# One transformer-style program: the first modulation's weights split into two float32r parts throughout, squares summed in pairs on GpSimd, five key units mixed into the start

## The reference, cut to what matters

```python
silu_c  = silu(c)                    # c: 1 x 2048
silu_cc = silu(c_ctx)[None]
mod_l = split(silu_c  @ w_mod + b_mod, 6)      # w_mod: 2048 x 12288, float32
mod_c = split(silu_cc @ w_mod + b_mod, 6)
hl = modulate(rms_norm(x,   norm1_g), mod_l[0], mod_l[1])
hc = modulate(rms_norm(ctx, norm1_g), mod_c[0], mod_c[1])
zl  = hl @ w_in + b_in                         # 256 x 13312
zkv = hc @ w_in[:, K_OFF:G_OFF] + b_in[K_OFF:G_OFF]   # keys and values of the context
```

## Time and profile before

| what | value |
|---|---|
| median of 3 runs | 2806.58 us (2803.66 to 2813.95) |
| the profiled execution, its own time | 2808.74 us |
| its span | 2806.9 us |
| mean granted TensorE clock | 0.981 |
| TensorE busy | 2705.8 us (96%), 21438 matmuls |
| VectorE busy | 1914.6 us (68%) |
| ScalarE busy | 1269.0 us (45%) |
| GpSimd busy | 188.1 us (7%) |

### The profile page before, as it was taken

One profiled execution on the slowest core, in us unless ns is written; L12 is line 12 of the kernel. 1 busy time (PEld: TensorE's weight loads), 2 busy tenths in 40 slices (PEclk: granted clock), 3 DMA queues, 4 the chain that ended last, 5 costly groups with the idle time before them and its releaser, 6 DMA issues.

```text
span 2806.9 us, 51478 instructions
## 1 busy us (share of the span) xinstructions
PE 2705.8 (96%) x21438; PEld 2581.1 (92%) x21438; DVE 1914.6 (68%) x2951; ACT 1269.0 (45%) x1827; POOL 188.1 (7%) x180
## 2 busy tenths in 40 slices
PE   7999999899999999999999999999999998979996
PEld 4599977798999999999999999999999998979996
DVE  6765667789998777875555645677566656487564
ACT  5522344553444545544443434464444444444453
POOL 0000011000014000100000000030000000220011
PEclk9999999999999999999999999999999999989998
DMA  8766633456876777776555555554344443535563
GB/s 310 270 229 222 204 115 112 143 188 205 273 239 223 248 265 263 258 255 205 183 191 183 181 192 183 188 187 152 135 155 146 151 150 128 175 104 180 181 200 108
DMA packets 163991, 539.02 MB, mean 192 GB/s; under 512 B 31024, under 2 KB 35120, under 8 KB 163632
## 3 DMA queue, kind: packets, MB, share of 16 engines
q1 hardware_dynamic: 163760, 535.73, 57.3%
HBM read 533.57 MB, written 2.10 MB: 191 GB/s over the span
## 4 chain that ended last, share of the span: by engine, by line
PE 62%; DVE 5%; issue 1%; ACT 1%; POOL 0%; POOLq 0%; ACTq 0%; DVEq 0%
PE ps L531 20%; PE ps L536 19%; PE ps L533 19%; DVE lo L1570 1%; DVE row L2137 1%; PE ps L865 0%; DVE AL L2213 0%; PE ps L887 0%; PE ps L888 0%; PE ps L569 0%; DVE H L2221 0%; DVE ON L2145 0%; DVE Z L2301 0%; PE ps L960 0%; PE ps L959 0%
## 5 line engine op out<-in xcount | busy, mean ns | idle before, releaser
L986 ACT ACTIVATE hi<-raw 128x1024 fp32r<-128x1024 f32 x856 | 902.0, 1059 | 954.3 <-PE ps L536 463.2
L531 PE MATMUL ps<-AH,hi 128*128 128x256 f32 (+2 forms) x4480 | 1283.5, 287 | 13.7 <-DVE AL L2213 13.7
L536 PE MATMUL ps<-AH,lo 128*128 128x256 f32 (+2 forms) x4480 | 1270.4, 284 | 9.5 <-DVE lo L1570 9.5
L533 PE MATMUL ps<-AL,hi 128*128 128x256 f32 (+2 forms) x4480 | 1269.4, 283 | 0.0
L1570 DVE TENSOR_TENSOR lo<-raw,hi 128x1024 fp32r<-128x1024 f32 x856 | 1036.0, 1224 | 201.3 <-ACT hi L986 198.9
L531 PEld LDWEIGHTS ps<-AH,hi 128*128 128x128 f32 x4480 | 850.4, 190 | 45.8 <-issue 34.6
L536 PEld LDWEIGHTS ps<-AH,lo 128*128 128x128 f32 x4480 | 849.9, 190 | 12.3 <-DVE lo L1570 12.3
L533 PEld LDWEIGHTS ps<-AL,hi 128*128 128x128 f32 x4480 | 851.2, 190 | 1.0
L531 PE MATMUL ps<-YH,hi 128*128 128x256 f32 (+1 forms) x1536 | 433.8, 282 | 6.5 <-DVE YL L2148 6.5
L536 PE MATMUL ps<-YH,lo 128*128 128x256 f32 (+1 forms) x1536 | 432.9, 282 | 0.0
L533 PE MATMUL ps<-YL,hi 128*128 128x256 f32 (+1 forms) x1536 | 432.5, 282 | 0.0
(11 more groups left out here) (253 smaller groups left out, 2493.2 us busy)
## 6 DMA issues: line engine op xcount, KB each, us to landing
raw<-in_w_ff SPq DMA_DIRECT2D x256, 512.0 KB, 4.1
raw<-in_w_in SPq DMA_DIRECT2D x208, 512.0 KB, 4.4
raw<-in_w_mod SPq DMA_DIRECT2D x192, 512.0 KB, 4.7
raw<-in_w_ain SPq DMA_DIRECT2D x128, 512.0 KB, 3.6
raw<-in_w_pin SPq DMA_DIRECT2D x64, 512.0 KB, 3.5
raw<-in_w_o SPq DMA_DIRECT2D x32, 512.0 KB, 4.7
raw<-in_w_aout SPq DMA_DIRECT2D x32, 512.0 KB, 3.5
raw<-in_w_pout SPq DMA_DIRECT2D x32, 512.0 KB, 4.3
```

The source lines that it names most:

```text
L531: e.matmul(b.ap[:, o], hi[:, k, :], xh, start=start and k + i == 0, stop=False, skip_group_check=many)
L533: e.matmul(b.ap[:, o], hi[:, k, :], xl, start=False, stop=False, skip_group_check=many)
L536: mm = e.matmul(b.ap[:, o], los[j % NSPLIT][:, k, :], xh, start=False, stop=stop and k == KU - 1, skip_group_check=many)
L986: e.activation(his[u % NSPLIT][:, :, :], raws[raw_at[i]][:, :].rearrange("p (k m) -> p k m", k=KU), ACT.Copy).then_inc(s_hi, 1)
```

## The change

1. `WHOLE` and the way `mod0` are gone: all 64 blocks of the first modulation are split in hi and lo and go through L639's form (L625 after the change). Every raw buffer of the start is freed by VectorE's `lo`.
2. GpSimd adds, for x and for ctx, the second square to the first and the fourth to the third (128x1024 each, new semaphore `s_sqa`). TensorE sums eight k tiles in place of sixteen. The place of the sums in TensorE's order moves from after the 6th to after the 10th block for x, and for ctx to after the 17th; the roots and reciprocals move with them.
3. `NLEAD` goes from 4 to 5 and `NEARLY` from 48 to 40: after 40 blocks w_in 40, 8 blocks, w_in 41, 8 blocks, w_in 42, 8 blocks, w_in 43, w_in 44, then the second halves of 40 to 44. The fifth unit accumulates in the bank `TB`, which the value transposes use later. `NSTART` is 69.

```diff
-WHOLE = (2, 5)
-NEARLY, NLEAD = 48, 4
+NEARLY, NLEAD = 40, 5
 NSTART = 64 + NLEAD
-FIRST = 64 - 8 * len(WHOLE) + NLEAD
+FIRST = NSTART
...
-    mod0 = [("mod0" if q in WHOLE else "mods", nb, q) for nb in MOD0 for q in range(8)]
+    mod0 = [("mods", nb, q) for nb in MOD0 for q in range(8)]
...
+        acc_kv = acc + [TB] + [acc[i % 4] for i in range(11)]
...
@@ TensorE, norms
-                    for _ in range(6 - 3 * c):
+                    for _ in range(9 - 3 * c):
                         yield
                     opened(xb)
-                    for k in range(16):
+                    for k in range(8):
                         if k % 4 == 0:
-                            e.wait_ge(s_sqx, 4 * c + k // 4 + 1)
-                        mm = e.matmul(XB[:, 0:T], ones[2048][:, :], squares[4 * c + k // 4][:, k % 4, :],
-                                      start=(k == 0), stop=(k == 15))
+                            e.wait_ge(s_sqa, 2 * c + k // 4 + 1)
+                        mm = e.matmul(XB[:, 0:T], ones[2048][:, :], squares[4 * c + k // 4 * 2][:, k % 4, :],
+                                      start=(k == 0), stop=(k == 7))
...
@@ TensorE, the start
-                if name == "mod0":
-                    e.wait_ge(*landed(i))
-                    for j in range(2):
-                        k = 2 * q + j
-                        mm = e.matmul(b.ap[0:2, :], vt[:, SC + 2 * k:SC + 2 * k + 2],
-                                      raws[raw_at[i]][:, 512 * j:512 * j + 512], start=False, stop=False,
-                                      skip_group_check=True)
-                    mm.then_inc(s_m0p, 1)
...
@@ ScalarE, norms
-                for key in ("x", "ctx"):
-                    root(rows[ROW[key] % 2], T)
-                    for _ in range(4):
-                        yield
+                yield
+                yield
+                root(rows[ROW["x"] % 2], T)
+                for _ in range(7):
+                    yield
+                root(rows[ROW["ctx"] % 2], T)
+                for _ in range(4):
+                    yield
...
@@ VectorE, norms
-                    for _ in range(8 if key == "x" else 1):
+                    for _ in range(10 if key == "x" else 2):
                         yield
...
@@ GpSimd
+            for i in (0, 2, 4, 6):
+                e.wait_ge(s_sqx, i + 2)
+                e.tensor_tensor(squares[i], squares[i], squares[i + 1], ALU.add).then_inc(s_sqa, 1)
```

More of the change, by code:

```diff
@@ L172, in unit_plan, with early_times @@
     return plan
-def early_times(plan, lead):
-    places = [i for i in range(NSTART) if plan[i][0] != "mod0"]
+def early_times(lead):
     at, n = [], 0
     for i in range(NSTART):
-        seen = sum(p <= i for p in places)
-        upto = min(len(places), seen + lead)
-        at.append(places[n:upto])
-        n = max(n, upto)
+        upto = min(NSTART, i + 1 + lead)
+        at.append(range(n, upto))
+        n = upto
     return at
@@ L364, in build @@
             sem(f"s_{n}") for n in ("tanh", "silu", "lamp", "lam", "lame", "setup"))
-        s_m0p, s_m0e, s_m0t, s_m0v, s_mx, s_hx, s_lx, s_cs, s_sqx = (
-            sem(f"s_{n}") for n in ("m0p", "m0e", "m0t", "m0v", "mx", "hx", "lx", "cs", "sqx"))
+        s_m0e, s_m0t, s_m0v, s_mx, s_hx, s_lx, s_cs, s_sqx, s_sqa = (
+            sem(f"s_{n}") for n in ("m0e", "m0t", "m0v", "mx", "hx", "lx", "cs", "sqx", "sqa"))
         s_k, s_vf, s_vt, s_vtok, s_q, s_mask, s_qk, s_bias, s_max, s_exp, s_pn, s_ptr, s_pta, s_ptv, s_av, s_na = (
@@ L405, in build @@
                 raw_free[i] = (s_mod, n_mod)
-            elif key[0] == "mod0":
-                n_m0p += 1
-                raw_free[i] = (s_m0p, n_m0p)
             else:
@@ L444, in block_in @@
                 name, m, h = plan[nxt]
-                src = ar["w_mod"][m, h] if name in ("mod", "mod0", "mods") else ar[name][m, h]
+                src = ar["w_mod"][m, h] if name in ("mod", "mods") else ar[name][m, h]
                 if before[nxt] is not None:
@@ L622, in _ @@
                     opened(b)
-                if name == "mod0":
-                    e.wait_ge(*landed(i))
+                unit_at += 1
+                u = unit_at
+                for part, ready in ((his, s_hi), (los, s_lo)):
+                    w = part[u % NSPLIT][:, :, :].rearrange("p k m -> p (k m)")
+                    e.wait_ge(ready, u + 1)
                     for j in range(2):
                         k = 2 * q + j
-                        mm = e.matmul(b.ap[0:2, :], vt[:, SC + 2 * k:SC + 2 * k + 2],
-                                      raws[raw_at[i]][:, 512 * j:512 * j + 512], start=False, stop=False,
+                        mm = e.matmul(b.ap[:, :], CS[:, 4 * k:4 * k + 128], w[:, 512 * j:512 * j + 512],
+                                      start=(q == j == 0 and part is his), stop=(q == 7 and j == 1 and part is los),
                                       skip_group_check=True)
-                    mm.then_inc(s_m0p, 1)
-                else:
-                    unit_at += 1
-                    u = unit_at
-                    for part, ready in ((his, s_hi), (los, s_lo)):
-                        w = part[u % NSPLIT][:, :, :].rearrange("p k m -> p (k m)")
-                        e.wait_ge(ready, u + 1)
-                        for j in range(2):
-                            k = 2 * q + j
-                            mm = e.matmul(b.ap[:, :], CS[:, 4 * k:4 * k + 128], w[:, 512 * j:512 * j + 512],
-                                          start=(q == j == 0 and part is his), stop=(q == 7 and j == 1 and part is los),
-                                          skip_group_check=True)
-                    mm.then_inc(s_unit, 1)
+                mm.then_inc(s_unit, 1)
                 if q == 7:
@@ L672, in _ @@
                 if m < NLEAD:
-                    unit(bank[m], KU, both, False, True, (lambda k: e.wait_ge(s_lx, 2 * k + 2)) if m == 0 else None)
-                    bank[m].free = (s_k, m + 1)
-                    tile_at = m + 1
+                    b = (bank + [tb])[m]
+                    unit(b, KU, both, False, True, (lambda k: e.wait_ge(s_lx, 2 * k + 2)) if m == 0 else None)
+                    b.free = (s_k, m + 1)
+                    tile_at = 0
                 else:
```

11 lines of the change are left out of this document (6 added, 5 removed).

## The result

The changed kernel takes 2816.41 us (median of 11 runs, 2813.44 to 2824.07), the kernel before beside it 2807.09 us (11 runs, 2801.99 to 2813.95). The ratio is 1.0033, 95% interval 1.0022 to 1.0045: slower by 9.3 us (6.2 to 12.6). The forecast was 2805.8, and the result lies 0.4 us above the range. Its profiled execution took 2819.71 us (span 2817.9; before 2808.74 and 2806.9).

The account below looks back on a forecast made before the run. TensorE was taken as the bound from 160 us and late in the start, where VectorE waits for its turns. Terms -4.8 + 4 = -0.8 us made the profiled 2808.74 into 2807.9, less 2.2 to the median: 2805.8; range 2791 to 2816.

Parts of the forecast that it names:

- the order of waits: Start, VectorE in series with TensorE's turns: last column at 149.1 us with four w_in halves done, gain 4.8 us.
- the clock: Start: TensorE falls to 1.2 GHz before ctx mean, w_in 40 or 42; cost 4 us, bounds 0 and 9.6.
- B: Rival, start: low clock at ctx mean, w_in 40, 42 and split bursts; net +4.8 to +7.8 us, 2811.4 to 2814.4; chance 0.25.
- C: Rival, start: GpSimd's adds take 11 us, so the sums come late; +5.2 us net, 2811.8; chance 0.05.
- a last column after 154 us: Sign, end of the start: B or C holds, told apart by the clock and the end of the adds.
- Whole blocks become split: Start: TensorE saves 13.6 us, VectorE gains 18.1 us of subtractions, ScalarE 16 copies; loads cost nothing.
- Squares in pairs: Sums of squares for x and ctx: TensorE saves 3.5 us twice; GpSimd's adds take 2.7 to 5.5 us, cost nothing.
- GpSimd gives way, VectorE does not: GpSimd adds beside VectorE splits: the split keeps its 1.22 us, the add stretches, taken as 5.5 us.
- The 1.8 us that the prediction worked out: Reciprocal for x at 40.0 us: pushed back if a split waits for the last ctx add; sum becomes +1.0.
- The fifth unit: Start: its first half, 5.4 us, can run while TensorE waits for the last modulation rows; no work added.
- walk: VectorE's new order through the start: reciprocal for x at 40.0, last five columns at 86.4, 102.9, 116.9, 135.0, 149.1 us.
- A: Rival, start: waits of 1.9, 3.5 and 2.4 us vanish and the clock holds; -12.6 us, 2794.0; chance 0.2.

Follow-up runs that it names:

- after_pieces: The changed kernel with each of GpSimd's four 128x1024 adds issued as four of 128x256; 2816.42 us, ratio 1.0030.
- no_pairs: The changed kernel without GpSimd's adds, TensorE again summing sixteen squares, at the new places; 2823.35 us, ratio 1.0050.
- filled: The changed kernel with a low-part matmul repeated as filler in 32 blocks of the start, where VectorE is slow; 2816.00 us, ratio 1.0024.

## Why the prediction was wrong

The number failed by 10.6 us, the sign too. The step that failed is the fourth, the order of waits, whose gain of 4.8 us was forecast and isn't there; the fifth, the clock, was right in kind and too small. The sign that the prediction had set for its rivals B and C, a last column after 154 us, came, and the clock tells it for B. By its steps:

1. *Whole blocks become split.* VectorE was busy 96.65 us where I had 95.6, and the loads cost nothing visible. The sizes were right. What they do together I had only half drawn: with this part alone the kernel is 6.2 us slower.
2. *Squares in pairs.* "GpSimd gives way, VectorE does not" failed. The adds took 2.46 to 3.13 us (bounds 2.7 to 5.5), but the splits beside them 2.64 and 3.31. I had one row, the split at 351.32 and the add at 351.36, and read it as a rank between engines. The split had begun 0.04 us earlier. What decides is who begins first, and after_pieces shows both orders. The rule that I set aside was right; the Trainium skill (SBUF — State Buffer, SBUF: two separate sides) says even this, that whichever starts first holds the shared ports for the whole instruction, and the traces agree. Its price here is small: at most the 0.9 to 1.5 us that after_pieces gained at the last column, and even that may be the shorter dip's. The 1.8 us that the prediction worked out by a line of the Trainium skill (Advanced Engine Details and Errata, where it stands under GPSIMD Details) needed a last add ending at 41.8; the adds ended at 22.6, 27.1, 32.7 and 37.1 us. The adds with their shorter sums are a gain for the changed kernel (no_pairs).
3. *The fifth unit* fills time in which TensorE waits. In the usual start of before there is hardly any: in the fourth profile TensorE is busy 102.0 of the 104.6 us to the last column. In the time it measured nothing: 1.0002 and 1.0000.
4. *The order of waits: gain 4.8.* This step failed, and twice. Its reference, the last column at 148.5, was the latest of six; against their mean of 145.4 the same walk gains 1.7. And the walk's own places came 9.1 us late in the mean of two profiles (158.2 against 149.1). Some 2 us of this are a step that it left out. Moving the sums put VectorE's first column and one split ahead of the reciprocal for x; before, the reciprocal came first (38.34, the column at 42.42). The walk began with the reciprocal at 40.0. The rows, of before, of after and of filled:

```profile
38.34 1.75 DVE L1650 RECIPROCAL row<-row 128x256 f32<-128x256 f32 x1 [2.46 <-ACT row L1016]
...
42.42 0.15 DVE L1668 TENSOR_TENSOR modv<-ps,vec 128x4 f32<-128x4 f32 x1
```

```profile
41.23 1.21 DVE L1562 TENSOR_TENSOR lo<-raw,hi 128x1024 fp32r<-128x1024 f32 x1
42.37 1.74 DVE L1642 RECIPROCAL row<-row 128x256 f32<-128x256 f32 x1
```

```profile
42.12 1.74 DVE L1646 RECIPROCAL row<-row 128x256 f32<-128x256 f32 x1
```

The turn for that column in after came only at 40.00 us, behind the sums, and the column at 41.09. With fillers, and with the adds in pieces (42.11), the reciprocal is as late, so this much is neither the clock nor GpSimd alone. From there on the walk's durations fit: after the seven splits and sixteen rows VectorE is at 57.4 us, 15.0 later.
5. *The clock: +4.* Right in kind: the dips lay where step 5 put them, on the ctx mean, w_in 40 and w_in 42. The fillers give back 4.2 to 4.8 us of the last column, and 20.5 us of the lower level were still left with them, so the whole price may be higher. In the first profile of after the lateness against the walk grows from 2.4 us at the reciprocal to 4.3, 6.5, 6.7, 8.7 and 8.8 at the last five columns, that is by some 2 us at each of the three dips and by 0.3 elsewhere.

So of the 9.1 us 2.1 are the walk's missing step and 4.2 to 4.8 are the clock as the fillers show it. Some 2.5 remain with the fillers in place; 1.9 of them come between the fourth and the fifth column, where w_in 40 still meets 3.4 us of the lower level (up to 1.7 us) and waits 1.3 us for its own split. That this is the clock too is argued from the place, not shown. With these sizes the start costs -1.7 (the gain against the usual start) + 2.1 + 4.5 + 2.5 = +7.4 us. The sum closes by construction, since its last term is the remainder. What it can be held against is the measured 9.3 us, whose interval (6.2 to 12.6) has 7.4 in it.

Of the rivals, A (-12.6) is out: the waits it wanted gone are there. B was right in mechanism, with 44.4 us of the lower level in place of 17.1, and its 2814.4 was the nearest of the cases. The page that spoke for it (the Trainium skill, TensorE: Matmul & The Clock Gate, A second HAM failure mode) was the better guide: by it B was the likelier case, and the trace agrees. C is out: in the profile after no add took more than 3.13 us, where C wanted 11, and all four had ended before the means that use them, which began at 34.8 and 53.7 us. The first add took 2.46 us and the third 2.47: of an extra cost of a first call there is no sign.

What I should have asked is whether the reference is stable. The profile held the hint. The dip at 97.6 us came with few gaps of TensorE around it: it was idle for 0.6 of the 4 us from 96 to 100. In the other executions of the same program, with little idle time there too, it came by half or not at all. The profile's total gave no warning, because the first profile was late at the start and lucky afterwards.

## What to carry to other kernels

Where a forecast is a difference of a few us in one stage, take the stage's times from several profiles of the same kernel: here one stage moved by 4.4 us between executions whose totals differed by 1. Work taken from TensorE while it stands in series with VectorE came back as idle time, and with the idle time came a lower clock for the next group that counts (30.7 us of it with split blocks alone, 13.7 to 17.1 before). When a step is moved, look at what now stands in front of it in each engine's order. A few matmuls without a purpose in the gaps shortened the start by 4 us, though what of that reaches the end has to be measured. And when one wait vanishes, look at the sum of the waits before counting it as won.

## What the runs showed of the hardware that was not expected

TensorE's 256-column matmuls follow each other at one of two steady intervals, near 113 or near 117 ns, over tens of us, both at the full granted clock and without a gap. The windows of 1290 to 1340 us, of before and of its second profile:

```profile
1290.00:1340.00 50.00, 50.00 (x443) 50.00 (x443) 25.39 (x28) 19.54 (x19) 0.00 (x0) 1.00 0.59 191
```

```profile
1290.00:1340.00 50.00, 50.00 (x427) 50.00 (x427) 23.89 (x28) 19.10 (x18) 0.00 (x0) 1.00 0.58 189
```

443 and 427 matmuls in 50 us of unbroken work. The third and the fourth profile have 444 each, and in 1110 to 1150 us the same four executions have 355, 342, 355 and 342. So the state is not fixed by the program. It changes mostly where a turn of the later modulation, a stall or a dip interrupts the stream, and doubling the matmuls of a turn didn't alter that. It moved the same kernel by up to 9 us between 500 and 1400 us (against the first profile: +6.2, +0.5 and +8.8 for the other three), and this explains most of the scatter of single profiles there: counted in blocks of twenty starts, the longer interval held for 286, 405, 276 and 478 us of that stretch in the four, which at 4 ns a start makes +4.3, -0.3 and +6.9 us of the three differences. What it is, and whether a kernel can choose the faster one, is open.

A short group is dear: a float32 matmul of a single column with weights of 128x128 takes 0.23 us of TensorE in two records, twice as long as a float32r one of 256 columns in a stream (0.113). And of a VectorE and a GpSimd instruction that each read two tensors, the second to begin stands still until the first has ended: at all four adds of the changed kernel the split beside it ended 1.08 or 1.09 us after the add.
